# One ring of eight tiles for the experts' weights, and router work reordered

## The reference

```
N_EXPERTS = 8; TOP_K = 2; D_FF_EXPERT = 3584; D_MODEL = 1024; SEQ = 256
# for every expert e and the tokens that chose it:
#   hid = silu(h @ w_gate[e]) * (h @ w_up[e])      (1024 -> 3584, twice)
#   y  += weight * (hid @ w_down[e])               (3584 -> 1024)
# then x = x + y, and a final RMS norm with the gain final_norm
```

## Time and profile before

| what | value |
| --- | --- |
| median of 3 runs | 2178.85 us |
| the profiled execution | 2182.77 us |
| its span | 2180.7 us |
| PE busy | 2114.9 us (97%) |
| the experts, first L1866 to the last L1882 | 1297.99 to 2167.5 us |
| DMA in the experts, 1332 to 2160 us | 414 GB/s, busy share 1.02 |
| queue q8, kind "instruction" | 89 packets, 1.46 MB |
| mean granted clock of PE | 0.988 |

### The profile page before, as it was taken

One profiled execution on the slowest core, in us unless ns is written; L12 is line 12 of the kernel. 1 busy time (PEld: TensorE's weight loads), 2 busy tenths in 40 slices (PEclk: granted clock), 3 DMA queues, 4 the chain that ended last, 5 costly groups with the idle time before them and its releaser, 6 DMA issues.

```text
span 2180.7 us, 67375 instructions
## 1 busy us (share of the span) xinstructions
PE 2114.9 (97%) x30418; PEld 1945.7 (89%) x30418; DVE 837.9 (38%) x2085; ACT 465.8 (21%) x1074; POOL 24.7 (1%) x43
## 2 busy tenths in 40 slices
PE   9999999999999999999997899999999999999998
PEld 8889999856999986899986789999999999999997
DVE  4357676314766655467759520101010101010102
ACT  3432112113311134211023221111111111111112
POOL 1000000000000000000000000000000000000000
PEclk9999999999999999999998999999999999999999
DMA  9241444240334423324431338999999999999997
GB/s 394 93 173 72 162 174 175 81 169 8 139 150 169 160 97 136 155 117 174 168 142 40 116 117 327 413 416 410 418 410 418 409 418 409 418 417 416 418 417 287
DMA packets 78407, 534.35 MB, mean 245 GB/s; under 512 B 9106, under 2 KB 9235, under 8 KB 41939
## 3 DMA queue, kind: packets, MB, share of 16 engines
q1 hardware_dynamic: 74450, 519.82, 59.3%
q0 software_dynamic: 3840, 12.85, 1.6%
HBM read 523.00 MB, written 9.63 MB: 244 GB/s over the span
## 4 chain that ended last, share of the span: by engine, by line
PE 65%; DMA 4%; DVE 2%; ACT 1%; issue 1%; DVEq 0%; SPq 0%; ACTq 0%
PE ps L1866 24%; PE ps L1224 12%; PE ps L1882 11%; PE ps L1266 7%; DMA slot<-in_w_moe 4%; PE ps L1141 4%; PE ps L1633 2%; PE ps L1616 1%; DVE scr L2549 0%; PE ps L1813 0%; PE ps L1157 0%; PE ps L1503 0%; PE ps L1489 0%; PE ps L1096 0%; PE ps L1570 0%
## 5 line engine op out<-in xcount | busy, mean ns | idle before, releaser
L1866 PE MATMUL ps<-scr,slot 128*64 128x88 f32 x14336 | 595.4, 241 | 11.1 <-issue 5.4
L1866 PEld LDWEIGHTS ps<-scr,slot 128*64 128x64 f32 x14336 | 562.8, 137 | 22.1 <-issue 12.4
L2698 DVE TENSOR_TENSOR scr<-scr,ps 128x88 f32<-128x88 f32 x224 | 55.1, 246 | 727.1 <-ACT scr L982 727.1
L1882 PE MATMUL ps<-scr,slot 128*64 128x88 f32 x7168 | 315.5, 239 | 1.9 <-issue 1.9
L1882 PEld LDWEIGHTS ps<-scr,slot 128*64 128x64 f32 x7168 | 292.0, 137 | 5.1 <-issue 5.1
L1266 PE MATMUL ps<-scr,slot 128*128 128x256 f32 x1056 | 237.6, 380 | 1.6 <-DVE scr L2369 1.6
L1266 PEld LDWEIGHTS ps<-scr,slot 128*128 128x128 f32 x1056 | 196.6, 191 | 26.0 <-DVE scr L2369 2.0
L982 ACT ACTIVATE scr<-ps 128x88 f32<-128x88 f32 x224 | 54.5, 243 | 743.8 <-PE ps L1866 743.8
L1224 PE MATMUL ps<-vtok,slot 128*128 128x128 f32 x1056 | 139.6, 275 | 0.0
L1224 PEld LDWEIGHTS ps<-vtok,slot 128*128 128x128 f32 x1056 | 128.8, 192 | 0.2
L1224 PE MATMUL ps<-vtok,proj 128*128 128x128 f32 x1056 | 128.7, 275 | 0.0
(11 more groups left out here) (412 smaller groups left out, 2058.4 us busy)
## 6 DMA issues: line engine op xcount, KB each, us to landing
slot<-in_w_moe SPq DMA_DIRECT2D x224, 1024.0 KB, 12.2
slot<-in_w_moe SPq DMA_DIRECT2D x224, 512.0 KB, 12.2
slot<-in_w_ffn SPq DMA_DIRECT2D x33, 3072.0 KB, 10.8
slot<-in_w_even_in SPq DMA_DIRECT2D x3, 3072.0 KB, 27.2
slot<-in_w_odd_qk SPq DMA_DIRECT2D x2, 3072.0 KB, 10.6
slot<-in_w_s_glu SPq DMA_DIRECT2D x2, 3072.0 KB, 11.9
slot<-in_w_odd_v SPq DMA_DIRECT2D x2, 2048.0 KB, 8.4
slot<-in_w_even_in SPq DMA_DIRECT2D x2, 1536.0 KB, 10.6
```

The costliest lines, as they stand in the source:

```text
L1866: m = pe.matmul(gate_up(j, k)[s:s + STRIP], w[:, o:o + STRIP], xg[:, c], start=c == 0, stop=c == KD - 1, skip_group_check=True)
L1882: m = pe.matmul(y_sum(d)[s:s + STRIP], w[:, o:o + STRIP], hid[j][:, 0:CAP], start=False, stop=False, skip_group_check=True)
L2698: dve.tensor_tensor(hid[f % 4][:, 0:CAP], gbuf[f % 4][:, 0:CAP], gate_up(f, 1), ALU.mult).then_inc(hid_ready, 1)
```

## The change

- The ring is of eight tiles (`RING = 8`), two in each of the four slots, and is refilled from tile 0 on. Each tile's two transfers go on one semaphore (`moe_loaded`), and both are issued when PE has done that tile's down. PE waits for both before the tile's up.
- What had its place in the two lead slots (`hrow`, `xl`, `returned`) lies in buffers that are no longer used elsewhere (`proj`, `yT`, `xbp`, `rgw`, `scr`). The two waits for `moe_free` ahead of the scatter (on DVE and POOL) are gone.
- PE's loops have eight tiles a pass. As 28 is no multiple of 8, two experts are written as one unit of seven passes, `two`: three in a loop, one pass cut in the middle by the change of expert, three in a loop, and the next change. It is written once for experts 0 and 1 (first pass in straight code), once as the body of a loop of two passes for experts 2 to 5, and once for experts 6 and 7 (last pass in straight code).
- The gather of expert 1's inputs comes after the first eight tiles.
- In the router, PE has four filler products (`busy`) where the gain row was, and makes the gain row after the place products; ACT takes the exponential ahead of the gain row.
- The dense path (not taken with these inputs) is written for two experts a pass.

```diff
-RING = 4
-GROUPS = FE_TILES // RING
+RING = 8
+GROUP = 4
+ROUNDS = EXPERTS * FE_TILES // RING
+TURNS = 2 * FE_TILES // RING
...
+            def load_tile(h, unit):
+                for o, n in ((0, UP), (UP, DOWN)):
+                    sp.dma_start(places[h][:, o:o + n], a["w_moe"][bass.ds(unit, 1), :, o:o + n].rearrange(
+                                     "o p n -> p (o n)")).then_inc(moe_loaded[h], 16)
 
             for h in range(RING):
...
-            last = EXPERTS * FE_TILES // RING - 1
-            sp.wait_ge(up_ready, 2 * (FT0["moe"] + RING) + 2)
-            load_up(0, 2 * RING)
-            with sp.Fori(2, last) as i:
+                sp.wait_ge(slot_free, left(tile_slots[h]))
+                load_tile(h, h)
+            with sp.Fori(1, ROUNDS) as i:
                 for h in range(RING):
-                    sp.wait_ge(up_ready, i * (2 * RING) + (2 * (FT0["moe"] + h - RING) + 4))
-                    load_up((h + 1) % RING, i * RING + (h + 1))
                     sp.wait_ge(moe_free, i * RING + h + 1)
-                    load_down(h, i * RING + h)
...
                 take_tokens(1)
+                act.wait_ge(rt["diff"], 2)
+                act.activation(tiny[:, GA:GA + 1, 0:2], tiny[:, GA:GA + 1, 0:2], ACT.Exp
+                               ).then_inc(rt["exp"], 1)
                 for b in range(2):
...
             def router():
                 pe.wait_ge(tile_taken, TILE0["s5_glu"] + 2 * KD)
-                for c in range(KD):
...
+                busy(4, 5)
                 pe.wait_ge(mo["sel"], 2)
...
-                def four(e, i, last=False, first=False):
+                def turn(p, i, k, tiles, inputs=None, wrapped=None, last=False):
 
                     def at(scale, plus):
-                        return e * (GROUPS * scale) + i * scale + plus
...
+                        return p * (TURNS * scale) + i * scale + (k * scale + plus)
+
+                    for j in tiles:
+                        if j + 1 < RING:
+                            up(j + 1, at(32, 32), inputs if j + 1 == GROUP else None)
                         elif not last:
-                            up(0, at(16, 16), at(2, 3))
-                        down(j, here, at(RING, FT0["moe"] + j + 1))
+                            up(0, at(32, 64), wrapped)
+                        down(j, at(RING, FT0["moe"] + j + 1))
...
+                def two(p, first, last):
+
+                    if first:
+                        turn(p, 0, 0, every)
+                        gather(1)
+                    with pe.Fori(1 if first else 0, 3) as i:
+                        turn(p, i, 0, every)
+                    turn(p, 0, 3, even, inputs_of(2 * p + 1))
+                    if first:
+                        pe.wait_ge(fin["rowtaken"], 2)
+                    if last:
+                        turn_place()
+                    change(2 * p, not last)
+                    turn(p, 0, 3, odd)
+                    with pe.Fori(0, 2 if last else 3) as i:
+                        turn(p, i, 4, every, wrapped=i * 4 + (p * (4 * FE_TILES // GROUP) + 21))
+                    if not last:
+                        change(2 * p + 1)
+
+                gather(0)
+                up(0, 32, 1)
+                open_sums(None)
+                two(0, True, False)
+                with pe.Fori(1, EXPERTS // 2 - 1) as p:
+                    two(p, False, False)
+                two(EXPERTS // 2 - 1, False, True)
+                turn(EXPERTS // 2 - 1, 2, 4, every, last=True)
```

More of the change, by code:

```diff
@@ L314, in build_program @@
         combined, first_copied = sem("combined"), sem("first_copied")
[L315 to L316 removed]
+        moe_loaded = [sem(f"moe_loaded{i}") for i in range(RING)]
         moe_free = sem("moe_free")
@@ L428, in build_program @@
         mix0 = {"even_out": 0, "odd_out": KD, "mla_o": 2 * KD}
[L430 to L447, removed]
+        tile_slots = [(len(LOADED) - SLOTS + h // 2) % SLOTS for h in range(RING)]
+        places = [slots[s][:, h % 2 * (UP + DOWN):(h % 2 + 1) * (UP + DOWN)]
+                  for h, s in enumerate(tile_slots)]
+        ups, downs = [x[:, 0:UP] for x in places], [x[:, UP:UP + DOWN] for x in places]
+        hrow = proj[:, 8:16].rearrange("p a n -> p (a n)").rearrange("p (g d) -> p g d", g=2)
+        xl = proj[0:CAP, 16:20].rearrange("p a n -> p (a n)")
+        returned = [yT[:, 4:8].rearrange("p a n -> p (a n)"),
+                    xbp[:].rearrange("p a n -> p (a n)")[:, 0:D],
+                    rgw[:].rearrange("p k j n -> p (k j n)"), part(34, 4)]
         where = part(25)[:, 16:64].rearrange("p (n c) -> p n c", c=8)
@@ L1724, in router @@
                           skip_group_check=True).then_inc(mo["pos"], 1)
-            def up_weights(e, f, first):
-                if first and f < RING:
-                    pe.wait_ge(slot_loaded[lead_slots[f // 3]], lead_loaded[f // 3])
-                    return lead_ups[f]
-                pe.wait_ge(moe_up_loaded[f % RING], e * (16 * GROUPS) + 16 * (f // RING))
-                return ups[f % RING]
-            def down_weights(e, f, first):
-                if first and f < RING:
-                    pe.wait_ge(slot_loaded[lead_slots[1]], lead_loaded[1])
-                    return lead_downs[f]
-                pe.wait_ge(moe_down_loaded[f % RING], e * (16 * GROUPS) + 16 * (f // RING))
-                return downs[f % RING]
+                for c in range(KD):
+                    m = pe.matmul(ps[:, 6 + c // 4, c % 4 * P:c % 4 * P + P],
+                                  v("final_norm", c).to_broadcast([P, P]), ident, start=True, stop=True,
+                                  skip_group_check=True)
+                    if c % 4 == 3:
+                        m.then_inc(fin["row"], 1)
             def experts_dense():
@@ L1906, in open_sums, with change @@
                                   skip_group_check=True)
-                gather(0)
-                gather(1)
-                up(0, None, 1)
-                open_sums(None)
-                four(0, 0, first=True)
-                with pe.Fori(1, GROUPS) as i:
-                    four(0, i)
-                turn_rows(16)
-                open_sums(2)
-                turn_sums(2)
-                with pe.Fori(1, EXPERTS - 2) as e:
-                    with pe.Fori(0, GROUPS) as i:
-                        four(e, i)
-                    turn_rows(e * 16 + 16)
+                def change(e, rows=True):
+                    if rows:
+                        turn_rows(e * 16 + 16)
```

116 lines of the change are left out of this document (31 added, 85 removed).

## The result

The changed kernel takes 2230.09 us (2226.18 to 2230.93, 4 runs) against 2179.67 (2175.48 to 2181.07, 4 runs) of the kernel before beside it: ratio 1.023, 95% interval 1.021 to 1.025. It is 50 us slower. The forecast was 2204, 24 to 25 us slower: the direction and the mechanism hold, the size is off by a factor of two, and 2230 lies 3 us above the range of 2186 to 2227 that the forecast gave for its own mechanism.

What follows compares the result with a forecast made beforehand. The weights' stream was taken to set the pace (3.80 us a tile against PE's 3.64). Last down 2132.5 + 54 + 6 = 2192.5, 25 us behind before; 25 added to the median 2178.85 gives 2204 us, range 2186 to 2227.

Steps and rivals of the forecast that it cites:

- first up: Start of the experts on PE: first up at 1294.8 instead of 1297.99, once the first half of `xg` is there.
- PE's own work: PE in the experts: 224 tiles x 3.64 = 815.4, sums' opening 0.5, late gather 2.4, seven expert changes 19.4 us.
- stops at packets: PE waiting for new code in the experts: 77 packets at 0.7 us each, 54 us.
- branch back: Outer loop's one branch back, between experts 3 and 4, to code that must be fetched: +6 us, bounds 2 to 9.
- last down: End of PE's expert work: 2132.5 + 54 + 6 = 2192.5, 25 us behind the 2167.5 of before.
- the price of a packet: Mean PE stop per code packet beside the full weights' stream in the experts: 0.7 us, bounds 0 and 2.7.
- its own term of -3.2 us: Start, router to first up: reordering makes the first up earlier; bounds -3.2 to +2 us.
- q8 at 159 packets: Sign on the code queue, whole page: some 155 packets instead of 89 if right, over 230 if loops are not kept.
- the first refills: Sign in the weights' ring: refills start near 1301 instead of 1314.66, following the first down, 13.4 us earlier.
- the rival at 2285: Eight-tile loops in the experts don't stay, each pass fetches its code again: 2285 us (2240 to 2345), chance 0.20.
- The rival in which the stream alone decides: In the experts PE's stops vanish in waits for weights, mean stop below 0.28 us: median 2171, chance 0.15.
- the new ring's intended gain of 8 us: Weights' stream alone, refilled 13.4 us earlier: last down near 2159.7 instead of 2167.5, 8 us gained.

Runs made afterwards that it cites:

- 1/16 of the weights: Changed kernel with each expert weight transfer cut to its first sixteenth of columns, PE's instructions kept: 2152.7 us, one run.
- the rings of seven: Changed kernel with seven ring tiles and one nest for experts 0 to 5, without and with expert 6 folded in: 2177.14 and 2177.19 us.

## Why the prediction was right in kind and wrong in size

The last down was forecast at 2192.5 and came at 2215.4 (first up 1295.49 + 919.95). Term by term:

| term | forecast, us | measured, us |
|---|---|---|
| first up | 1294.8 | 1295.5 |
| PE's own work | 837.7 | 841.3 (846.0 with 1/16 of the weights, less 4.7 at its seam) |
| stops at packets | 54 | 69, as the rest (920.0 - 841.3 - 9.6) |
| branch back | 6 | 9.6 (5.50 + 4.16, less two usual pitches) |
| last down | 2192.5 | 2215.4 |

**The step that failed is the price of a packet, 0.7 us for each of 77.** The runs show 69 / 77 = 0.90 as the mean. Of the 69 us, 64 can be read directly: 55 stops of 0.3 us and more from record to record, apart from the seam and one wait for DVE, 1.16 us on average; the rest lies in shorter gaps. A single stop was priced well. By the "issue" waits it is 1.03 us on average in the kernel before (7 waits) and 1.04 in the changed one (50 outside the seam). What the forecast had wrong is how many packets have one: 7 of the 19 that start in the expert phase before, 50 of 88 after, the seam's two left out. In a run of new code each packet costs 6.2 to 6.3 us from stop to stop (3.9 until it starts, 1.0 to carry it, 1.4 until PE goes on) against 4.83 us of work. The forecast had this in its hand: it read 6.01 us for 127 records off and used it for one stop, then averaged over 12 packets that came in loops of three (the trace has 15 beside the full stream). In each of those four first passes no stop of 0.4 us or more stands behind the last packet, it seems because the pass turns back before it is needed. The changed kernel's runs are two to three times as long, so that share of free packets didn't carry over. At 1.2 us for 55 of the 77 the sum would have been 66. This step is 15 of the 23 us.

**The branch back** was priced as one fetch, 6 us; it is two in a row. The first packet at the target holds only 19 records of the up, and the next one starts only 3.1 us after PE has gone on, so it wasn't on its way while PE stood. With the code 60 records further it is one fetch of 5.29, and the four branches back of the kernel before with experts 1 to 5 written out cost one each, 5.1 to 5.5. So one fetch was priced about right and the second was missed: 9.6 us, past the upper bound of 9, 3.6 more than forecast.

PE's own work gives another 3.6: at the half clock behind the seam, which stands in the run with 1/16 too, 64 records take some 2.4 us longer, and one change of expert has a wait of 1.0 us for DVE. The start gives 0.7, all of it from what lies ahead of the router in this execution; its own term of -3.2 us came out as said against this execution of the kernel before (12.8 to 9.6 us from the logits). The remaining 3 us between 2204 and 2230 are not the change's: the profiled execution of before (2182.77) was 3.9 us over the median that the forecast started from (2178.85), that of the changed kernel (2230.93) 0.8.

**Right:** q8 at 159 packets (155 said), stops every 127 or so records and only in straight code and first passes, no waits for weights, the first refills by 1302.65 (1301.3 said), DMA share 0.99 in the experts (0.98 said). The loops of eight tiles do stay, so the rival at 2285 falls. The rival in which the stream alone decides, below 0.28 us a packet, falls for the changed kernel with 0.90. Its number can be held against the rings of seven, in which the stream does decide. It said 2159.7 for the last down with the first up at 1294.8, a phase of 864.9; they take 869.0 and 869.1. That one of them ends at 2159.9 is luck, since its first up came at 1290.9. So the new ring's intended gain of 8 us isn't there: against the kernel before with the new router order alone its phase is 2.7 us shorter, and the medians are the same (2177.1).

The Trainium skill calls the crossing of a 16 KiB border "mostly hidden" (Runtime: NRT & Kernel Launch, Instruction fetch mechanics). The trace agrees at 0.13 DMA share and not at 0.99; which it is depends on the data traffic beside it.

## What to carry over

Code is traffic. Where an engine works through a 16 KB packet of its code faster than the fetch takes beside a saturated stream, each packet of new code can cost the difference (here 6.2 to 6.3 us against 4.83), and a longer loop body bought for a deeper buffer can cost more than the buffer gives. Price such stops from the distance between two of them in a long run of new code, not from the mean over short loops, and ask of each loop how many packets it spans; choose a ring length that divides the loop (28 = 4 x 7), so that the code can stay. When a stream is the bound anyway, neither fewer stops nor a deeper ring need show in the time, as the two rings of seven did not.

## What was not expected of the hardware

- What code packets cost in all is nearly all or nothing: the phase is 6 us longer at a DMA share of 0.69 than at 0.13, 20 at 0.94, 74 at 0.99. The single fetch is not: at the seam the first one takes 2.67, 4.46, 5.77 and 5.50 us.
- The wait until a code packet starts doesn't shrink with the length of the weights' descriptors (3.88 and 3.85 us), and transfers of 2 KB per partition make the kernel some 20 us slower in its one run, at a share of 1.04 with only 381 GB/s:

```profile
1350.00:2120.00 770.00, 705.26 (x17972) 694.06 (x17969) 65.74 (x227) 104.05 (x231) 5.69 (x11) 0.99 1.04 381
```

- The two fetches at the seam run beside full engines, though the row of 1764 to 1774 above has a share of 0.55. That is a mean over a full and an empty part: the stream that was queued goes on while PE stands, until after the second packet has started at 1768.23, and only then do the engines run dry (share 0.05 from 1770 to 1775).

```profile
1760.00:1769.00 9.00, 1.72 (x19) 1.47 (x20) 0.88 (x2) 0.00 (x0) 0.51 (x1) 0.72 0.98 361
```

- A nest of two loops with 5.7 packets of code turns back for nothing; one of 19 packets is fetched again and costs one or two fetches at the branch, by where the packet border falls behind its target: 5.3 us or 9.6 under full traffic, and 4.8 (2.67 and 2.15) for the two with the engines nearly idle.
